# Turning a transformer layer's hidden rows: from TensorE transposes to reloads and VectorE's 32x32 blocks

## What is computed

```python
def pool_mixer(x, w_in, w_group, scale, w_out):
    u = (x @ w_in).reshape(b, t, N_POOL_GROUPS, POOL_GROUP)
    ...                                      # pooled: trailing means over 2, 4, 8, 16 tokens
    y = jnp.einsum('btgc,gce->btge', pooled - u, w_group).reshape(b, t, D_MODEL)
    return (y * scale) @ w_out

m = pool_mixer(h, a_w_in[j], a_w_group[j], a_scale[j], a_w_out[j])
h = layer_norm(ALPHA * h + m, ln_mix_g[i], ln_mix_b[i])
h = layer_norm(ALPHA * h + swiglu_ffn(h, ffn_w_gu[i], ffn_w_down[i]), ln_ffn_g[i], ln_ffn_b[i])
```

## Time and profile before

| | |
|---|---|
| median of 3 runs | 1639.8 us (1639.79, 1639.8, 1641.46) |
| the profiled execution | 1641.42 us, span 1639.6 us |
| TensorE busy | 1629.3 us, 99% of the span |
| VectorE busy | 1043.1 us, 64% |
| GpSimd busy | 640.4 us, 39% |
| ScalarE busy | 606.8 us, 37% |
| mean granted clock of TensorE | 0.998 of full |

### The profile page before, as it was taken

The page is one execution under the profiler, slowest core; times in us unless marked ns, Lnnn a source line. Parts: engine busy times, 40 slices in busy tenths (PEclk is TensorE's granted clock), DMA queues, the critical chain, the costliest instruction groups (busy, mean ns, idle before and its releaser), DMA issues.

```text
span 1639.6 us, 18911 instructions
## 1 busy us (share of the span) xinstructions
PE 1629.3 (99%) x7233; PEld 1349.7 (82%) x7233; DVE 1043.1 (64%) x1095; ACT 606.8 (37%) x837; POOL 640.4 (39%) x440
## 2 busy tenths in 40 slices
PE   9999999999999999999999999999999999999998
PEld 7888878888888888888888888888888888888886
DVE  7758756888445565554756777667544443467866
ACT  6225443545434434433533333333333332322330
POOL 0420025016358677664456765666720000341000
PEclk9999999999999999999999999999999999999999
DMA  9563456434367666556756666666577544564542
GB/s 365 201 253 132 154 201 235 163 146 179 116 200 235 204 209 226 195 195 210 254 194 206 211 197 199 210 214 187 177 242 257 189 147 140 199 218 167 205 142 95
DMA packets 192010, 322.45 MB, mean 197 GB/s; under 512 B 7856, under 2 KB 135984, under 8 KB 183216
## 3 DMA queue, kind: packets, MB, share of 16 engines
q1 hardware_dynamic: 152224, 289.25, 51.7%
q10 hardware_dynamic: 37520, 23.60, 4.6%
q0 software_dynamic: 2176, 8.39, 1.3%
HBM read 218.97 MB, written 102.24 MB: 196 GB/s over the span
## 4 chain that ended last, share of the span: by engine, by line
PE 98%; DVE 1%; ACT 0%; DMA 0%; issue 0%; DVEq 0%; SPq 0%; ACTq 0%
PE acc L1262 44%; PE acc L1292 19%; PE acc L1101 10%; PE turn L1262 7%; PE acc L1135 7%; PE turn L1292 6%; PE turn L1135 3%; PE acc L1167 1%; PE acc L1180 0%; PE turn L1090 0%; DMA raw<-w_out 0%; DVE sums L1743 0%; ACT st_mix L1340 0%; DVE mov L1703 0%; PE acc L1191 0%; DVE z L2146 0%
## 5 line engine op out<-in xcount | busy, mean ns | idle before, releaser
L1262 PE MATMUL acc<-fa,wf 128*128 128x512 f32 x1584 | 362.8, 389 | 0.0
L1262 PE MATMUL acc<-fb,wf 128*128 128x512 f32 x1584 | 362.8, 389 | 0.0
L1262 PEld LDWEIGHTS acc<-fa,wf 128*128 128x128 f32 x1584 | 297.3, 188 | 61.7
L1262 PEld LDWEIGHTS acc<-fb,wf 128*128 128x128 f32 x1584 | 297.4, 188 | 61.6
L1292 PE MATMUL acc<-dw,da 128*128 128x512 f32 x1386 | 315.3, 389 | 0.0
L1292 PEld LDWEIGHTS acc<-dw,da 128*128 128x128 f32 x1386 | 260.2, 188 | 53.9
L1883 DVE TENSOR_TENSOR wf<-wt,wf 128x512 fp32r<-128x512 f32 x132 | 134.2, 1020 | 139.7 <-ACT wf L1477 139.7
L1883 DVE TENSOR_TENSOR wf<-wr,wf 128x512 fp32r<-128x512 f32 x176 | 187.4, 1071 | 38.9 <-ACT wf L1477 38.5
L927 POOL TENSOR_TENSOR wt<-wr,wt 128x512 f32<-128x512 f32 x88 | 140.8, 1600 | 150.8 <-DVE wf L1883 150.6
L1477 ACT CAST wf<-wr 128x512 fp32r<-128x512 f32 x176 | 108.6, 618 | 214.6 <-PE acc L1262 211.8
L1101 PE MATMUL acc<-mov,split 128*128 128x512 f32 x768 | 179.5, 393 | 0.0
(11 more groups left out here) (152 smaller groups left out, 1809.1 us busy)
## 6 DMA issues: line engine op xcount, KB each, us to landing
wr<-w_gu SPq DMA_DIRECT2D x44, 1024.0 KB, 5.2
dar<-af_dram SPq DMA_DIRECT2D x56, 704.0 KB, 4.5
af_dram<-g ACTq DMA_DIRECT2D x32, 512.0 KB, 5.7
fs<-hf_dram SPq DMA_DIRECT2D x14, 1024.0 KB, 5.6
dt_raw<-w_down SPq DMA_DIRECT2D x22, 512.0 KB, 5.8
wt_dram<-dt_t SPq DMA_DIRECT2D x22, 512.0 KB, 3.7
sa<-af_dram SPq DMA_DIRECT2D x22, 512.0 KB, 8.3
af_dram<-sx SPq DMA_DIRECT2D x22, 512.0 KB, 4.5
```

The costliest lines, as they stand in the source:

```text
L1262: mm = nc.tensor.matmul(dst, wf[:, slot, a, k, :], fa[half][i][:, v, :, k, :], start=i < 2 and k == 0 and n3 == 0, stop=k == KC - 1 and n3 ...
```

## The change

The first half's pairs are turned as the second half's are. `load_pair` reloads them from `h_dram` into the very `zm` tiles they were stored from: per pair and block four DMAs of 128 KB, each behind the store of its rows, 32 in all, placed in SyncE's queue between the stores of the first half and the z loads. VectorE turns a pair with four transposes of 128x512 in `turn_pair`, for pairs 0 and 1 behind the poolings in its steps p1 and p2, for pairs 2 and 3 ahead of the poolings in its steps p4 and p5. (In its step p, VectorE pools step p - 1.) ScalarE scales in place with `scale_turned`, eight instructions of 128x256 a pair as before, now all in its steps p2 to p5. TensorE's `turn_part` and the waits for it are gone. ScalarE normalizes all four rows of block 1 in its step p0, before two were in p0 and two in p1. In SyncE's queue `load_in(1, 2)` moves ahead of `load_x(3, 2)`, and `load_z` and `load_mix` take other turns.

```diff
--- before.py
+++ after.py
@@ -410,17 +410,17 @@
...
-        def pair_rows(pi, a, kk):
-            return zm[a][:, pi].rearrange("p (r c) -> p c r", c=KT)[:, kk]
+        def pair_place(pi, a):
+            return zm[a][:, pi].rearrange("p (g n) -> p g n", g=QT) if pi < TT else nat_gu[:, a]
...
-        def turned_block(n):
+        def turned_block(pi, n):
             a, kh = ((1, 0), (0, 0), (0, 1), (1, 1))[n]
-            src = nat_gu[:, a].rearrange("p g (r c) -> p g c r", c=KT)[:, :, kh * KC:(kh + 1) * KC]
-            return st_gu[:, n].rearrange("p k (g t) -> p g k t", t=Q), src
+            src = pair_place(pi, a).rearrange("p g (r c) -> p g c r", c=KT)[:, :, kh * KC:(kh + 1) * KC]
+            return st_of(pi)[:, n].rearrange("p k (g t) -> p g k t", t=Q), src
@@ -608,11 +608,14 @@
                             sp.wait_ge(rows_stored[e][row], 2 * 16)
+                elif pi > TT:
+                    sp.wait_ge(turn_done, TT * pi)
                 else:
-                    sp.wait_ge(turn_done, TT * pi)
+                    sp.wait_ge(rows_stored[a][pi], 16)
                 src = h_dram.rearrange("(h a j g t) (q c) -> h j a g q t c", h=2, a=2, j=TT, g=QT, q=QT)[half, j, a]
                 for n in range(QT):
-                    sp.dma_start(nat_gu[:, a, n], src[n]).then_inc(pair_landed[a], 16)
+                    sp.dma_start(pair_place(pi, a)[:, n], src[n]
+                                 ).then_inc(z_landed[a][pi] if pi < TT else pair_landed[a], 16)
@@ -792,22 +795,30 @@
                 store_h(0, j)
+            load_in(1, 2)
+            load_pair(0, 0)
+            load_pair(1, 0)
             load_x(3, 2)
                 store_h(1, j)
-            load_in(1, 2)
+            load_pair(0, 1)
+            load_pair(1, 1)
+            load_pair(2, 0)
+            load_pair(2, 1)
+            load_in(1, 3)
+            load_pair(3, 0)
+            load_pair(3, 1)
             load_z(2, 0)
             load_z(3, 0)
-            load_in(1, 3)
             load_z(2, 1)
             load_z(3, 1)
+            load_mix(1, 0)
             load_z(2, 2)
             load_z(3, 2)
-            load_mix(1, 0)
+            load_mix(1, 1)
             load_z(2, 3)
             load_z(3, 3)
-            load_mix(1, 1)
             load_mix(1, 2)
@@ -1079,18 +1090,7 @@
...
-            def turn_part(pi, k):
-                part = TT * pi + k
-                if k == 0:
-                    pe.wait_ge(normed, TT + pi + 1)
-                if part >= 2:
-                    pe.wait_ge(turn_taken, 2 * (part - 1))
-                for n, (a, kk) in enumerate(((1, k), (0, k), (0, KC + k), (1, KC + k))):
-                    mm = nc.tensor.transpose(turn[:, k % 2, n * P:(n + 1) * P], pair_rows(pi, a, kk), ident[:])
-                mm.then_inc(turn_done, 1)
-            def hidden(c, x_of, slot, banks, before=None, between=None):
+            def hidden(c, x_of, slot, banks, before=None):
                 chunk_is_split(c)
@@ -1103,8 +1103,6 @@
                         mm.then_inc(chunk_done, 1)
-                    if between is not None:
-                        between(m)
@@ -1116,7 +1114,6 @@
                         pe.wait_ge(added, added_by(h - 1, 4, m))
-                        pe.wait_ge(turn_taken, 2 * TT * TT)
                     elif t == 1:
@@ -1212,12 +1209,7 @@
...
-                    def turn_two(m):
-                        turn_part(p - 1, 2 * m)
-                        turn_part(p - 1, 2 * m + 1)
-                    hidden(c_in(h, i), mov_of(b), c_in(h, i) % 2, p % 2, x_is_split if first and p == 0 else None,
-                           turn_two if h and 1 <= p <= TT else None)
+                    hidden(c_in(h, i), mov_of(b), c_in(h, i) % 2, p % 2, x_is_split if first and p == 0 else None)
                     if first:
@@ -1246,7 +1238,7 @@
                     if n == 0:
-                        pe.wait_ge(turn_taken, 2 * TT * TT)
+                        pe.wait_ge(added, added_by(LAST_HALF, 4, 2))
                     else:
@@ -1323,27 +1315,6 @@
...
-            def take_turn(pi, k):
-                part = TT * pi + k
-                act.wait_ge(turn_done, part + 1)
-                if k == 0 and pi < 2:
-                    act.wait_ge(d_lo_ready, NP)
-                if k == 0 and pi >= 2:
-                    act.wait_ge(st_stored[pi % 2], 16 * (pi // 2))
-                    act.wait_ge(ss_made, 4 * (pi - 1))
-                if part == 0:
-                    act.wait_ge(mix_gb_kept, 1)
-                for n, kk in enumerate((k, KC + k)):
-                    nc.scalar.activation(st_of(pi)[:, 2 * n:2 * n + 2, k, :],
-                                         turn[:, k % 2, 2 * n * P:2 * (n + 1) * P].rearrange("p (b t) -> p b t", t=P),
-                                         ACT.Identity, bias=mix_b_sb[:, kk:kk + 1], scale=mix_g_sb[:, kk:kk + 1]
-                                         ).then_inc(turn_taken, 1)
-                if k == KC - 1:
-                    store_turned(pi)
             def store_turned(pi):
@@ -1352,8 +1323,10 @@
                 act.wait_ge(turn_done, TT * pi + 3 + kh)
+                if pi == 0:
+                    act.wait_ge(mix_gb_kept, 1)
                 for k in range(KC):
-                    both, kk = st_gu[:, 2 * kh:2 * kh + 2, k, :], kh * KC + k
+                    both, kk = st_of(pi)[:, 2 * kh:2 * kh + 2, k, :], kh * KC + k
                     nc.scalar.activation(both, both, ACT.Identity, bias=mix_b_sb[:, kk:kk + 1],
@@ -1494,19 +1467,16 @@
                     if h and 2 <= p <= TT + 1:
-                        take_turn(p - 2, 2)
-                        take_turn(p - 2, 3)
-                    if h and 1 <= p <= TT:
-                        take_turn(p - 1, 0)
-                        take_turn(p - 1, 1)
+                        scale_turned(p - 2, 0)
+                        scale_turned(p - 2, 1)
                     if p >= 6:
...
                         x_hi(2 * h + 1, 2 * p + 1)
-                    if h and p < 2:
-                        norm(1, 2 * p)
-                        norm(1, 2 * p + 1)
+                    if h and p == 0:
+                        for j in range(TT):
+                            norm(1, j)
@@ -1788,7 +1758,7 @@
                     if t in (1, 3):
-                        dve.wait_ge(z_landed[t // 3][m], 16 * (h + 1))
+                        dve.wait_ge(z_landed[t // 3][m], 16 * (1 + (QT + 1) * h))
                     out_is_done(dve, h, t, m)
@@ -1883,6 +1853,19 @@
...
+            def turn_pair(pi):
+                if pi < 2:
+                    dve.wait_ge(d_lo_ready, NP)
+                else:
+                    dve.wait_ge(st_stored[pi % 2], 16 * (pi // 2))
+                    dve.wait_ge(ss_made, 4 * (pi - 1))
+                for step, n in enumerate(TURN_ORDER):
+                    if step % 2 == 0:
+                        dve.wait_ge(z_landed[1 - step // 2][pi], 16 + 16 * QT)
+                    dst, src = turned_block(pi, n)
+                    nc.vector.transpose(dst, src).then_inc(turn_done, 1)
             def mixer_block(h):
@@ -1905,8 +1888,12 @@
                             dve.wait_ge(fold_stored[n], 16 * GROUPS)
+                    if h and p in (4, 5):
+                        turn_pair(p - 2)
                     if p >= 1:
                         pool(2 * h + STEPS[p - 1][0], STEPS[p - 1][1])
+                    if h and p in (1, 2):
+                        turn_pair(p - 1)
                     if p == 6:
@@ -1995,7 +1982,7 @@
                     dve.wait_ge(pair_landed[0], 16 * QT * (pi - TT + 1))
-                dst, src = turned_block(TURN_ORDER[step + place])
+                dst, src = turned_block(pi, TURN_ORDER[step + place])
                 nc.vector.transpose(dst, src).then_inc(turn_done, 1)
```

## The result

The changed kernel takes 1645.82 us (median of 6 runs, 1645.21 to 1647.25), the one before 1639.88 (6 runs, 1639.79 to 1642.03). The ratio is 1.0035, interval 1.0022 to 1.0048: slower by 0.35%, where 1634.3 us and a gain were forecast. It lies outside the forecast range, on the side of rival D. The profiled execution has a span of 1644.0 us, 4.4 above that of before.

What follows compares the result with a forecast made beforehand. TensorE bounds the kernel (99% busy); -11.3 us of transposes + 2.9 waiting + 2.1 lower clock = -6.3 us, giving 1635.1 from the profiled execution, 1633.5 from the median, middle 1634.3; range 1628.5 to 1641.0 us.

Steps and rivals of the forecast that it cites:

- rival D: Slower, chance 0.15: every pair's store lands like the 10.9 us one, VectorE sets t1 to t3; 1645 halfway, 1651 at bounds.
- The same form is in the trace, 596 ns in the middle: SyncE: the added 128 KB reload DMAs take 596 ns each, as the same form does in the trace.
- I cost the queue at nothing: SyncE's queue: reloads out by about 234; the loads behind them not needed by TensorE before 289, so no cost.
- the 2.1 us for the lower clock: TensorE after its wait at p7: the lower granted clock loses 2.1 us more.
- First `pair_sums`: GpSimd: starts at about 234.9, after pair 0's turn and eight scalings, 1.3 us later than before.
- Landings: Stores of the first two pair_sums: 10.9 us each, from the trace's range of 4.8 to 10.9.
- Wait of p7: TensorE before the product p7: starts at 281.0, waiting 2.9 us for ScalarE's staging of p5.
- The 11.3 us of TensorE: Eight hidden products of the second half: without transposes 87.1 us instead of 98.4, 11.3 us removed if nothing else waits.
- The order of the gates: Before p7: the third pair_sums frees pooling p4, that frees ScalarE's staging of p5, and that frees p7.
- x halves in time: VectorE's last x_lo ends at 221, needed by p2 at 223.7: slack 2.7 us.
- The slack of 1.2 us for p4's weights: VectorE's split of p4's weights ends at 244.2, needed at 245.4.
- the store at 287.2: GpSimd's pair_sums 3 ends at 287.2; its store lands near 293.6, and pooling p6 then ends at 298.9.

Runs made afterwards that it cites:

- By quarter: Changed kernel with its reloads cut into one DMA per quarter of the features, outermost length 32 in place of 4: 1634.93 us, ratio to before 0.9962.
- with the z loads last: Changed kernel with reloads cut per quarter of the features and all eight z loads moved behind the first two outward weights: 1637.65 us, ratio 0.9985.
- with two tiles as well: Changed kernel with reloads cut per quarter of the features and a second ss_mix tile for odd pairs: 1632.2 us, ratio 0.9957.

## Why the prediction was wrong

**The step that failed** is SyncE's: "The same form is in the trace, 596 ns in the middle" and "I cost the queue at nothing". The form was the same, but the earlier trace rows give the issue of a DMA, not its transfer, and during the second half's reloads nobody waits for them. What the reload moves per microsecond was never read, though the trace of before has it: 90 to 98 GB/s behind a group of four. 24 in a row of 128 KB each at that rate need 33 us, not 14. In place of 596 ns the runs show 1268, and in place of a landing "near 224" one at 230; of these 6 us, 2 came ahead of the reload, since the store of its rows landed after 7.0 us. By quarter the issue costs 434 ns, and the time is 1634.93, 0.6 us from the forecast. That closeness is in part luck: the profiled execution lacks the 2.1 us for the lower clock, and took 1633.09 where 1635.1 was forecast for it.

**What it set off**, in the prediction's own chain. First `pair_sums`: forecast 234.9; measured 237.57, and 234.63 by quarter. Landings: forecast 10.9 and 10.9; measured 12.0 and 14.1, and 11.9 and 10.4 by quarter. The queue was to be out "by about 234" and held until 260, so ScalarE's stores, z loads and weights that should have spread stand beside the second landing. Start of pooling p4: forecast 274.4, measured 282.55, and 274.23 by quarter. Wait of p7: forecast 2.9, measured 9.25, and 2.74 by quarter.

**What held.** The turning: 4.27 us a pair, forecast 4.6. The 11.3 us of TensorE: steps p0 to p3 run at 10.92. The order of the gates: GpSimd's third sums, pooling p4, staging p5, p7. The lower clock behind p7's wait: 13.14 us for 10.9, forecast 2.1 more. The granted clock (third number from the end, as a share of full) is at its lower level, 1.2 GHz, in the first 4 us:

```profile
289.04:291.04 2.00, 2.00 (x5) 1.61 (x6) 1.70 (x4) 2.00 (x2) 0.00 (x0) 0.50 0.15 61
291.04:293.00 1.96, 1.96 (x6) 1.53 (x5) 1.96 (x1) 1.96 (x2) 0.77 (x1) 0.50 0.03 10
```

x halves in time: p2 doesn't wait.

**What was short.** The slack of 1.2 us for p4's weights, by 0.45 us, since VectorE had waited 2.52 us for pair 0's reload; and that of p5's, by 0.97, since w_in took 13.9 us to land beside the reloads and the first two pairs' stores. One sum doesn't come out: the store at 287.2 with a landing of 4.8 gives 292.0, not 293.6; the forecast time doesn't hang on it.

**Rival D** is what happened, through another cause than it named. It was to decide once pooling p6 ends later than 306.4; pooling p6 ended at 310.6, and its rule, t3 26.5 us behind that, gives 337.1, where t3 starts near 337.15. The wait stands at t1, though, whose form VectorE finishes at 315.0; that both come out alike is no proof of the rule (with the z loads last it gives 327.4, and t3 starts near 328.9). Its halfway time, 1645, is near what was measured (1645.82), but not by its cause, every store landing after 10.9 us: they landed after 12.0, 14.1, 9.3 and 4.6. It had 0.15, because the landings were given a spread and the reload none. VectorE's load as the cause of long landings isn't borne out: with half of its turning time gone stores still landed after 12.1 and 12.7 us, and with the z loads away, and the turning kept, one landed in 5.5 us.

**Not settled.** That crowding makes a landing long was shown for the first store only, by moving the z loads; for the second one's 14.1 us it is argued. The lower clock behind p7's wait isn't there in each profile: by quarter, 48 matmuls took 11.18 us at full clock behind 2.74 of waiting; with two tiles as well 13.78 behind 3.21, its first 4 us at half clock. That may be part of the scatter of these kernels (some 4 us); it wasn't tried. That the issue of a DMA goes at the pace of the transfers in a long row, and not in a group of four, is read from the times; what holds it back wasn't tried.

## What to carry to other kernels

Read a transfer's rate in GB/s and the share of the engines beside its issue time, before an off-path transfer is put on a path: a transfer nobody waits for hides a factor of 2.6. Of two ways to cut the same bytes, look at the outermost length on both sides: here 32 moved 250 GB/s and 4 moved 96. When a step moves, the next gate is likely a tile or a store that was never late, so follow the whole chain of who frees what, and price VectorE and GpSimd side by side.

## What of the hardware was not expected

- The same pieces of 1 KB moved at 49, 96 and 250 GB/s with outermost lengths of 2, 4 and 32, with 2, 4 and about 16 tiny packets for each DMA; issuing slowed with them, 1.46 us for 64 KB (46.82 / 32), 1.22 for 128 KB (19.44 / 16) and 0.53 for 128 KB (8.53 / 16), and held back all behind it in the queue.
- A 1 MB store of GpSimd landed after 5.5 us beside a weight and ScalarE's store, and after 11.9 beside the same and z loads; after 4.6 us with little else (by quarter, the third store).
- One VectorE instruction of 1.22 us took 5.12 beside four of GpSimd's, three of which kept their 1.3 us.
